# A two-layer hybrid encoder on one core: the first head's Q and K prepared earlier, weight splits and one-column products moved into the attention loop

## The reference

```python
D_MODEL, SEQ, DEPTH = 1024, 512, 2
for l in range(DEPTH):
    mod = (c_act @ w_ada[l] + b_ada[l])[:, None, :]
    sh_a, sc_a, g_a, sh_m, sc_m, g_m = jnp.split(mod, 6, axis=-1)
    h = x * (1.0 + sc_a) + sh_a
    proj = h @ w_in[l]
    a_q, a_k, a_v, b_cq, b_ckv, b_kr, c_q, c_k, c_v = jnp.split(proj, IN_SPLITS, axis=-1)
    y_a = dilated_mixture(...)      # A: 4 heads, 3 window patterns, relative bias
    y_b = mla_attention(...)        # B: 4 heads, Q and K, V from compressed cq and ckv, rotary key shared
    y_c = axial_gqa(...)            # C: 8 query heads on 2 key/value heads
    y = jnp.concatenate([...], -1) @ w_o[l]
    x = layer_norm(ALPHA * x + (1.0 + g_a) * y, ln1_g[l], ln1_b[l])
    h = x * (1.0 + sc_m) + sh_m
    y = jnp.square(jax.nn.relu(h @ w1[l])) @ w2[l]
    x = layer_norm(ALPHA * x + (1.0 + g_m) * y, ln2_g[l], ln2_b[l])
```

## Time and profile before

| | |
|---|---|
| median of 3 runs | 1390.79 us (1390.37 to 1392.11) |
| the profiled execution | 1388.87 us |
| its span, first to last instruction | 1387.1 us |
| PE busy | 1317.0 us, 95% |
| DVE, ACT, POOL busy | 992.6, 602.3, 329.2 us |
| mean granted TensorE clock | 0.988 |

### The profile page before, as it was taken

One profiled execution on the slowest core, in us unless ns is written; L12 is line 12 of the kernel. 1 busy time (PEld: TensorE's weight loads), 2 busy tenths in 40 slices (PEclk: granted clock), 3 DMA queues, 4 the chain that ended last, 5 costly groups with the idle time before them and its releaser, 6 DMA issues.

```text
span 1387.1 us, 19960 instructions
## 1 busy us (share of the span) xinstructions
PE 1317.0 (95%) x6888; PEld 1113.3 (80%) x6888; DVE 992.6 (72%) x1673; ACT 602.3 (43%) x1258; POOL 329.2 (24%) x427
## 2 busy tenths in 40 slices
PE   4899889999999999999999998899999999999995
PEld 2899777788978788888879987678898788888884
DVE  6668889975799778667774747999478855534577
ACT  0447479962631232222235657798152232222321
POOL 0013056641215000000020505966040700000005
PEclk9999999999999999999999998999999999999998
DMA  8863600004456445653224340000236233323332
GB/s 294 303 207 108 235 28 1 28 16 121 124 175 220 142 165 200 215 185 122 95 80 134 98 129 14 1 28 1 91 97 230 86 97 99 97 94 97 98 99 91
DMA packets 88167, 164.55 MB, mean 119 GB/s; under 512 B 8025, under 2 KB 18649, under 8 KB 88081
## 3 DMA queue, kind: packets, MB, share of 16 engines
q1 hardware_dynamic: 87408, 161.08, 35.4%
q10 hardware_dynamic: 672, 2.36, 0.5%
HBM read 159.21 MB, written 4.19 MB: 118 GB/s over the span
## 4 chain that ended last, share of the span: by engine, by line
PE 64%; DVE 17%; DMA 6%; ACT 5%; POOL 4%; issue 3%; SPq 1%; POOLq 0%; ACTq 0%; DVEq 0%
PE bank L1558 20%; PE bank L1559 20%; PE bank L1560 20%; DVE ada_sum L968 4%; PE bank L1786 2%; DMA slab_raw<-in_w_in 2%; DVE pt_lo L1223 1%; DVE smax L1210 1%; DMA slab_raw<-in_w 1%; PE bank L1589 1%; DVE slab_lo L1325 1%; DVE h_lo L1333 1%; DVE sqr L1331 1%; POOL prob L558 1%; ACT pt_hi L851 1%
## 5 line engine op out<-in xcount | busy, mean ns | idle before, releaser
L1558 PE MATMUL bank<-hT_hi,slab_hi 128*128 128x512 f32 (+1 forms) x640 | 235.9, 369 | 0.0
L1560 PE MATMUL bank<-hT_hi,slab_lo 128*128 128x512 f32 (+1 forms) x640 | 235.4, 368 | 0.0
L1559 PE MATMUL bank<-hT_lo,slab_hi 128*128 128x512 f32 (+1 forms) x640 | 235.4, 368 | 0.0
L1325 DVE TENSOR_TENSOR slab_lo<-slab_raw,slab_hi 128x512 fp32r<-128x512 f32 x240 | 176.2, 781 | 82.4 <-ACT slab_hi L910 60.1
L1558 PE MATMUL bank<-slab_hi,h_hi 128*128 128x512 f32 x512 | 200.1, 391 | 3.7 <-DVE slab_lo L1325 2.0
L1560 PE MATMUL bank<-slab_hi,h_lo 128*128 128x512 f32 x512 | 199.3, 389 | 0.0
L1559 PE MATMUL bank<-slab_lo,h_hi 128*128 128x512 f32 x512 | 199.2, 389 | 0.0
L1558 PE MATMUL bank<-slab_hi,hT_hi 128*128 128x384 f32 (+3 forms) x448 | 152.8, 341 | 4.9 <-issue 1.7
L520 POOL TENSOR_SCALAR mv<-mv 128x1 f32<-128x1 f32 x16 | 5.5, 345 | 640.0 <-DVE mv L1271 639.3
L1012 DVE TENSOR_TENSOR slab_lo<-slab_raw,slab_hi 128x512 fp32r<-128x512 f32 (+3 forms) x144 | 81.3, 587 | 99.5 <-ACT slab_hi L628 99.3
L1559 PE MATMUL bank<-slab_lo,hT_hi 128*128 128x384 f32 (+3 forms) x448 | 151.2, 337 | 0.0
(11 more groups left out here) (203 smaller groups left out, 2552.4 us busy)
## 6 DMA issues: line engine op xcount, KB each, us to landing
slab_raw<-in_w SPq DMA_DIRECT2D x256, 256.0 KB, 2.8
ada_w<-in_w_ada SPq DMA_DIRECT2D x48, 1024.0 KB, 6.1
slab_raw<-in_w_in SPq DMA_DIRECT2D x48, 192.0 KB, 5.0
slab_raw<-in_w_o SPq DMA_DIRECT2D x32, 256.0 KB, 2.6
slab_raw<-in_w_in SPq DMA_DIRECT2D x16, 256.0 KB, 2.7
band<-bias_rows SPq DMA_DIRECT2D x8, 448.0 KB, 3.5
slab_raw<-in_w_in SPq DMA_DIRECT2D x16, 144.0 KB, 3.5
X<-in_x SPq DMA_DIRECT2D x1, 2048.0 KB, 9.7
```

What stands on the lines that cost most here:

```text
L1325: dve.tensor_tensor(slab_lo[:, slot, :], slab_raw[:, slot, :], f32(slab_hi[:, slot, :]), ALU.subtract).then_inc(slab_lo_done, 1)
L1558: pe.matmul(dst, a_hi, w_hi, start=first, stop=False)
L1559: pe.matmul(dst, a_hi, w_lo, start=False, stop=False)
L1560: return pe.matmul(dst, a_lo, w_hi, start=False, stop=last)
```

## The change

In both layers:

- ACT's `prepare_k(0)` and `prepare_q(0)` stand behind `uq`'s evacuation and before `uk`'s. For this k_hi, k_lo and q_lo have other addresses.
- `bv` writes banks 6, 7, 4, 5. PE waits there for `tkv`'s evacuation, and for `uk`'s from the third tile on. The first score waits no more for all of `bv`'s evacuation; the first transposes do.
- DVE's four writes to `qB` (L1166) stand in steps 0 to 3 of the attention loop, behind the maximum.

In the second layer ACT's splits of slabs 54 and 55 come before `uq`'s evacuation, DVE's before the products with the rotary table.

In the first layer:

- The loads of the last six halves of `w_ada` are all issued behind slab 47, ahead of slabs 48 to 55.
- DVE does the 32 `ada` steps of blocks 2 to 5 without splits between them (four of them earlier, behind the first two splits of `aqk`).
- Both engines' splits of slabs 48 to 55 stand in steps 4 to 11 of the attention loop: ACT's behind the exponential of that step, DVE's behind the maximum of that step.
- The one-column products stand in steps 64 to 67 of PE's loop, ACT's evacuation of them in step 69.

```diff
--- before.py
+++ after.py
@@ -52,8 +52,9 @@
 AHEAD = 4
 
 
-ADA_LOADS = {7: [0], 8: [1], 13: [2], 17: [3], 24: [4], 26: [5], 50: [6], 51: [7], 52: [8], 53: [9], 54: [10],
-             55: [11]}
+ADA_LOADS = {7: [0], 8: [1], 13: [2], 17: [3], 24: [4], 26: [5], 47: [6, 7, 8, 9, 10, 11]}
+
+WO_SPLITS_FROM = 4
 
 NOW = 6
 
@@ -194,9 +195,9 @@
         vC = over("vC", [P, TT, 128], 43008)
 
         q_hi = over("q_hi", [P, 2, S], 45056, F32R)
-        q_lo = over("q_lo", [P, 2, S], 49152, F32R)
-        k_hi = over("k_hi", [P, 2, S], 53248, F32R)
-        k_lo = over("k_lo", [P, 2, S], 57344, F32R)
+        q_lo = over("q_lo", [P, 2, S], 57344, F32R)
+        k_hi = over("k_hi", [P, 2, S], 49152, F32R)
+        k_lo = over("k_lo", [P, 2, S], 53248, F32R)
         v_hi = over("v_hi", [P, 2, TT, HD], 61440, F32R)
         v_lo = over("v_lo", [P, 2, TT, HD], 63488, F32R)
         pt_hi = over("pt_hi", [P, 2, TT, 256], 65536, F32R)
@@ -241,7 +242,8 @@
         LOW, HIGH = bank[:4], bank[4:]
         EVEN = [bank[i] for i in (0, 1, 4, 5)]
         ODD = [bank[i] for i in (2, 3, 6, 7)]
-        SETS = {"lnp": LOW, "lnq": LOW, "ad0": LOW, "adm": [bank[7]], "wo0": ODD, "wo1": EVEN, "lnr": ODD, "lns": ODD, "w1": EVEN}
+        SETS = {"lnp": LOW, "lnq": LOW, "ad0": LOW, "adm": [bank[1]],
+                "bv": [bank[i] for i in (6, 7, 4, 5)], "wo0": ODD, "wo1": EVEN, "lnr": ODD, "lns": ODD, "w1": EVEN}
 
         def banks(job):
             name = JOBS[job][0]
@@ -777,8 +779,9 @@
                                    scale=colpack[:, 32 + b:33 + b]).then_inc(bT_hi_done, 1)
                 for k in range(5, 8):
                     split(40 + k, 512)
-                for k in range(6):
-                    split(48 + k, 512)
+                if l > 0:
+                    for k in range(6):
+                        split(48 + k, 512)
 
                 slab_job_done(A_QK)
                 for b in range(4):
@@ -791,13 +794,35 @@
                 for h in range(4):
                     ins = act.activation(kB[64:96, h, :], banks(JOB["tkv"])[2][0:32, :], ACT.Copy)
                 ins.then_inc(evac_act, 1)
+                if l > 0:
+                    for k in range(6, 8):
+                        split(48 + k, 512)
                 for b in range(2):
                     act.wait_ge(bank_ready, l * B_LAYER + ready_before("uq") + b + 1)
                     src = banks(JOB["uq"])[b]
                     act.activation(qB[0:64, 2 * b, :], src[0:64, :], ACT.Copy, scale=SC_B)
                     evac(qB[0:64, 2 * b + 1, :], src[64:128, :], scale=SC_B)
-                for k in range(6, 8):
-                    split(48 + k, 512)
+                def v_src(i):
+                    m, h = HEADS[i]
+                    if m == "C":
+                        return vC[:, :, 64 * (h // 4):64 * (h // 4) + 64]
+                    return (vA if m == "A" else vB)[:, :, 64 * h:64 * h + 64]
+
+                def prepare_k(i):
+
+                    ks, ksrc, for_hi, _ = head_k(i)
+                    for at, to in for_hi:
+                        ins = act.activation(k_hi[to, ks, :], ksrc[at, :], ACT.Copy)
+                    ins.then_inc(k_hi_done, 1)
+
+                def prepare_q(i):
+                    s, qs, at, _ = head_q(i)
+                    act.activation(q_hi[at, s, :], qs[at, :], ACT.Copy).then_inc(head_hi, 1)
+
+                act.wait_ge(bank_ready, l * B_LAYER + ready_before("uq") + 4)
+                act.wait_ge(evac_act, a_at(l, "uk"))
+                prepare_k(0)
+                prepare_q(0)
                 for b in range(2):
                     act.wait_ge(bank_ready, l * B_LAYER + ready_before("uk") + b + 1)
                     src = banks(JOB["uk"])[b]
@@ -807,30 +832,7 @@
                     act.wait_ge(bank_ready, l * B_LAYER + ready_before("bv") + t + 1)
                     evac(vB[:, t, :], banks(JOB["bv"])[t][:, 0:256])
 
-
-                def v_src(i):
-                    m, h = HEADS[i]
-                    if m == "C":
-                        return vC[:, :, 64 * (h // 4):64 * (h // 4) + 64]
-                    return (vA if m == "A" else vB)[:, :, 64 * h:64 * h + 64]
-
-                def prepare_k(i):
-
-                    ks, ksrc, for_hi, _ = head_k(i)
-                    for at, to in for_hi:
-                        ins = act.activation(k_hi[to, ks, :], ksrc[at, :], ACT.Copy)
-                    ins.then_inc(k_hi_done, 1)
-
-                def prepare_q(i):
-                    s, qs, at, _ = head_q(i)
-                    act.activation(q_hi[at, s, :], qs[at, :], ACT.Copy).then_inc(head_hi, 1)
-
                 act.wait_ge(evac_act, a_at(l, "adm"))
-                prepare_k(0)
-                prepare_q(0)
-                if l == 0:
-                    mods_evac()
-                act.wait_ge(evac_act, a_at(l, "wo0"))
                 act.wait_ge(evac_dve, l * D_LAYER + d_before("wo0"))
                 for s in range(ATT_STEPS):
                     if s < UNITS:
@@ -842,6 +844,10 @@
                         act.activation(prob[:, s % 4, :], src, ACT.Exp, bias=smax[:, s % 4, 0:1],
                                        scale=-1.0 if m == "A" else 1.0, accum_out=smax[:, s % 4, 1:2]
                                        ).then_inc(exped, 1)
+                    if l == 0 and 0 <= s - WO_SPLITS_FROM < 8:
+                        split(48 + s - WO_SPLITS_FROM, 512)
+                    if l == 0 and s == UNITS + 5:
+                        mods_evac()
                     u = s - T_LAG
                     if 0 <= u < UNITS:
                         act.wait_ge(transposed, l * UNITS + u + 1)
@@ -1122,6 +1128,9 @@
                 dve.tensor_tensor(kr, t1, t2, ALU.add).then_inc(kr_roped, 1)
                 for k in range(2):
                     split(40 + k, 512)
+                if l == 0:
+                    for k in range(4):
+                        ada(2, k)
                 for b in range(2, 4):
                     dve.wait_ge(bank_ready, l * B_LAYER + ready_before("tc") + b - 1)
                     dve.tensor_copy(qC[:, b, :], banks(JOB["tc"])[b][:, :]).then_inc(evac_dve, 1)
@@ -1139,36 +1148,36 @@
                     dve.tensor_tensor(u_lo[:, j, :], u_raw[:, j, :], f32(u_hi[:, j, :]), ALU.subtract
                                       ).then_inc(up_lo_done, 1)
 
-                def split_and_ada(k):
-                    split(48 + k, 512)
-                    if l == 0:
-                        for n in range(3 * k, 3 * k + 3):
-                            ada(3 + n // 8, n % 8)
-
                 if l == 0:
-                    for k in range(8):
-                        ada(2, k)
-                for k in range(4):
-                    split_and_ada(k)
+                    for n in range(4, 16):
+                        ada(2 + n // 8, n % 8)
+                else:
+                    for k in range(4):
+                        split(48 + k, 512)
                 for b in range(2):
                     dve.wait_ge(bT_hi_done, l * 5 + 3 + b + 1)
                     dve.scalar_tensor_tensor(out=ckvT_lo[:, b, :], in0=banks(JOB["tkv"])[b][:, :],
                                              scalar=colpack[:, 35 + b:36 + b], in1=f32(ckvT_hi[:, b, :]),
                                              op0=ALU.mult, op1=ALU.subtract).then_inc(evac_dve, 1)
-                for k in range(4, 6):
-                    split_and_ada(k)
+                if l == 0:
+                    for n in range(16):
+                        ada(4 + n // 8, n % 8)
+                else:
+                    for k in range(4, 8):
+                        split(48 + k, 512)
                 for b in range(2):
                     dve.wait_ge(bank_ready, l * B_LAYER + ready_before("uq") + 2 + b + 1)
                     ins = dve.tensor_tensor(tmp[:, b, :], banks(JOB["uq"])[2 + b][:, :], ropeT[:, b, :], ALU.mult)
                     ins.then_inc(evac_dve, 1)
-                dve.wait_ge(evac_dve, l * D_LAYER + d_before("uk"))
-                for h in range(4):
+
+                def rope_of_q(h):
+
+                    if h == 0:
+                        dve.wait_ge(evac_dve, l * D_LAYER + d_before("uk"))
                     ins = dve.tensor_tensor(qB[64:96, h, :], tmp[32 * h:32 * h + 32, 0, :],
                                             tmp[32 * h:32 * h + 32, 1, :], ALU.add)
-                step(ins)
-                for k in range(6, 8):
-                    split_and_ada(k)
-
+                    if h == 3:
+                        step(ins)
 
                 def v_src(i):
                     m, h = HEADS[i]
@@ -1209,6 +1218,10 @@
                         else:
                             dve.tensor_reduce(smax[:, s % 4, 0:1], bank[s % 3][:, :], AX.X, ALU.max, negate=True
                                               ).then_inc(maxed, 1)
+                    if s < 4:
+                        rope_of_q(s)
+                    if l == 0 and 0 <= s - WO_SPLITS_FROM < 8:
```

(51 more changed lines are left out.)

## The result

The changed kernel takes 1402.61 us (median of 4 runs, 1402.26 to 1406.29) against 1390.58 us before; the ratio is 1.0091, with a 95% interval of 1.0079 to 1.0103. It is slower by 12.0 us in the medians, and by 13.4 in the spans (1400.5 against 1387.1). The prediction had 1401.6, slower. That the medians agree within 1.0 us is partly luck: the profiled execution took 1402.26 us where the sum gave 1399.7, so the sum was 2.6 us short, and the 1.9 us between a profiled execution and the median, added by the prediction, came out at 0.35 in the changed kernel.

A forecast was written before the change was run, and what follows sets the result against it. PE (busy 95%) and DVE (72%) were two near-bounds, DVE's part read as a chain. -5.1 + 1.2 + 15.3 + 3.3 - 3.9 = +10.8 us on 1388.87 gave 1399.7, plus 1.9 for the median 1401.6; range 1393 to 1408.

The forecast's parts named there:

- The ring of steps 4 to 11: First layer's attention: DVE's maximum, ACT's exponential and split, DVE's split and pt_lo form a loop, 3.27 us a step; +15.3 us.
- only DVE's work counts: Rival for steps 4 to 11: ACT's splits done before DVE asks, +4.3 in place of 15.3, 1390.6 us; 9%.
- everything lies under PE: Rival: PE sets the step and DVE's and ACT's splits fill gaps; sum -4.5, 1386.3 us; 6%.
- The first score of the first layer: Ahead of the first layer's attention: DVE's chain sets the first score at 176.1, 5.1 us earlier than 181.21.
- The one-column products: Steps 64 to 69, first layer: 32 records take 3.7 us, counted as +3.3; 0 if waits for pt_lo hid them.
- The second layer's first score: Second layer's start: the 3.90 us wait goes, qB's 1.2 us offset by the clock; -3.9, bounds -2.7 and -5.1.
- the writes to qB in steps 0 to 3: Attention start, both layers: DVE's four writes at 0.70 us now follow the first score; +1.2 us.
- POOL first: Rival for steps 4 to 11: POOL's scaling starts before DVE's split, which waits up to 0.69 us; +5.5, 1407; 10%.
- The clock: Rival: clock stays at 1.2 GHz for 4 to 8 us after step 11; +2 to +4, 1404 to 1406; 10%.

The follow-up runs named there:

- experiment 1: Changed kernel with DVE's splits of slabs 48 to 55 one step later (steps 5 to 12) than ACT's: 1392.38 us, ratio 1.0020.
- experiment 7: Changed kernel with DVE doing pt_lo before the split of the same step in steps 4 to 11: 1398.92 us, ratio 1.0065.
- Experiment 8: Changed kernel, splits at attention's end, qB writes before the loop, one-column products mostly before first score, DVE's K and Q before last eight ada steps: 1380.54 us.
- experiment 4: Changed kernel with the one-column products and their evacuation ahead of the first score again, out of steps 64 to 69: 1399.39 us, ratio 1.0068.
- Experiment 3: Changed kernel with DVE's four writes to qB ahead of the attention loop, not in steps 0 to 3: 1398.07 us, ratio 1.0057.

## Why the prediction was right

**The ring of steps 4 to 11** was the deciding term, and it came out at 28.20 us against the 28.2 worked out, 15.3 above before. Its parts match: 0.72, 0.67, 0.65, and 0.6 for each of DVE's instructions, 3.26 us where the sum had 3.27. That it is a ring and not load is shown twice: one step of distance between ACT's and DVE's split takes 10.8 us away with the same work (experiment 1), and moving `pt_lo` into the wait takes away 0.6 us a step (experiment 7). The rival "only DVE's work counts" has its size in experiment 1, 4.5 us; it would have been right for that kernel. (Its 4.3 took the 0.54 us that DVE had free in 7 us for the whole stretch; in 12.9 us it is 1.0, which gives 3.8. The measured 4.5 holds about 1.0 us of POOL's.) The rival "everything lies under PE" fell with the same run: there is no room even for 4.5 us.

**The first score of the first layer** came 5.2 us earlier (5.1 predicted), by the steps named: `ckvT_lo` at 157.2, a wait for the load ended at 166.66, Q done at 176.4. Seen from the transposes of ckv every mark is within 0.2 us of the sum; one wait of 0.39 us for a load (at 170.16) was not foreseen. PE waited 6.95 us, "about 7". Experiment 8 shows DVE as the cause: with K and Q ahead of eight `ada` steps the first score no longer waits for DVE.

**The one-column products** cost 3.2 us at the end of the loop by experiment 4, against 3.3 (the 2.8 us of the table hold whatever else changed there); and nothing ahead of the first score, where PE waits anyway.

**The second layer's first score** came 4.1 us earlier, with PE at its full clock: its first matmul took 0.40 us as foreseen, with no wait in front. The layer's whole gain was 2.9 and not 3.9 us, near the bound of 2.7, for the reason that follows.

```profile
856.37 0.40 PE L1785 MATMUL bank<-k_hi,q_hi 128*128 128x512 f32 x1
```

**What was mis-sized: the writes to qB in steps 0 to 3.** I counted 0.70 us each and +1.2 us in the first layer, and set 1.2 against a gain by the clock in the second. Measured were +2.7, and in the second layer +1.6 from the first score to the maximum of step 4 (6.81 to 8.44). Experiment 3 parts that: with the writes out of these steps and the clock full it is 5.73 us, so the better clock gives about 1.1 us, near the 1.2 that I had set, and the writes cost 2.7, not 1.2. The row was in my hands, and I used it only for the splits. DVE's instructions with both inputs in SBUF take longer when POOL's scaling has started before them. POOL's timeline in the changed kernel beside the DVE rows above:

```profile
180.06 1.09 POOL L560 TENSOR_SCALAR prob<-prob,smax 128x512 f32<-128x512 f32 x1
...
182.19 0.69 POOL L560 TENSOR_SCALAR prob<-prob,smax 128x512 f32<-128x512 f32 x1
...
183.93 0.69 POOL L560 TENSOR_SCALAR prob<-prob,smax 128x512 f32<-128x512 f32 x1
...
187.76 1.07 POOL L560 TENSOR_SCALAR prob<-prob,smax 128x512 f32<-128x512 f32 x1
```

At 182.32 and 184.16 POOL was first (182.19, 183.93): POOL took its 0.69 us, DVE's writes 1.10 and 1.00 and not 0.68. POOL's scaling at 180.06 was itself held up by the write at 179.91, and then held up the Q at 180.60. At 187.58 DVE's split was first (POOL 187.76): DVE took 0.69, POOL 1.07. That is the order that the prediction had for the splits, all eight times, so the rival "POOL first" did not happen; POOL's longer scaling lies outside the ring. By the Trainium skill (SBUF — State Buffer, "Who interferes with whom") the port that the two share is an exclusive lock, and the order of issue decides who waits. These rows agree with it, for an instruction on 32 partitions too.

With 0.4 us more for the Q (1.08) and 0.4 and 0.3 more for two of the writes (1.10 and 1.00) the start of the first layer comes to +2.3 of its +2.7 us; the rest is 0.1 us in each of the four steps: from a maximum to the write behind it took 0.71 to 0.73 us, where 0.61 was counted.

**The clock** was a rival with 10%. Windows of the changed kernel (columns as in the earlier trace rows) show the granted clock at 0.50 in the ring and again right behind it:

```profile
188.00:192.00 4.00, 1.09 (x4) 0.71 (x4) 2.64 (x5) 2.33 (x6) 2.37 (x3) 0.50 0.01 2
192.00:196.00 4.00, 3.82 (x16) 3.52 (x17) 2.57 (x5) 1.78 (x4) 1.52 (x3) 0.50 0.00 0
...
204.00:208.00 4.00, 1.96 (x15) 1.82 (x16) 2.58 (x4) 1.81 (x6) 1.62 (x2) 1.00 0.00 0
...
212.00:216.00 4.00, 2.73 (x11) 2.43 (x12) 3.94 (x7) 3.20 (x7) 1.78 (x3) 0.50 0.00 0
216.00:220.00 4.00, 4.00 (x23) 3.62 (x22) 3.70 (x6) 2.19 (x6) 2.55 (x4) 0.69 0.01 2
```

It did not change a step of the ring (3.26 us at either level, DVE's idle time 1.36 or 1.37 in all eight). Behind it PE had steps at the low clock until about 218, but step 12 to w_o is only 2.8 us longer, and experiment 4, with the one-column products out of it, is 0.4 us shorter than before there. That fits a lower clock paid for by the lead that PE had over DVE, as the prediction set them against each other, but it is argued: no run parts the two.

## What to carry to other kernels

When two in-order engines share a piece of work (one makes the high part, the other the low part), look where it stands in both queues relative to every other thing they exchange: in the same step, behind a hand-over in the other direction, it closes a ring and costs its latency on top of its busy time (10.8 and 4.5 us here). One step of distance removes the latency; a place where the engine waits anyway removes nearly all of the work as well. Before making an early start earlier, ask which queue stands behind it: here a wait of PE for DVE came in place of three others, and giving PE work in that wait (experiment 4) or taking work off DVE's head (experiments 3 and 8) was what paid.

## What the hardware showed beyond that

A DVE instruction on only 32 partitions (`qB`, 0.68 us alone) was held up by POOL about as much as the Q on 64 (1.00 and 1.10 us against 1.08), and it held up POOL as much as a split on 128 did (1.09 us at 180.06, 1.07 at 187.76). In all these rows, and in the three splits of experiment 1, the later one ends 0.53 to 0.56 us after the earlier one's end, whatever its size in partitions. Which of the two waits is decided, in the ring, by less than 0.2 us (187.58 against 187.76).

A low clock cost time only where PE set the pace. The changed kernel went from the first maximum to the maximum of step 4 in 7.77 us in both layers, with the granted clock at 0.50 for the first 3 us of it in the first layer and at 1.00 throughout in the second: DVE, with the writes to `qB`, set it. In the second layer of experiments 1 and 4 the clock was at 0.50 for 3.4 us of these same steps, and the stretch stayed at 143.4 and 143.3 us (143.4 in the changed kernel). In experiment 8, without the writes in these steps, as long a low clock went with 1.0 us more.
